# A hybrid decoder step in split fp32: halves of the seven-product matmul regrouped, state transposes and forget loads moved

## What is computed

```
x = x + 0.5 * SwiGLU1(RMSNorm(x))          # (silu(x @ w_gate) * (x @ w_up)) @ w_out, hidden width 2816
h = RMSNorm(x); z = h @ w_in               # q|k|v|forget logits, RG-LRU inputs, short-conv inputs, 3 branch gates
o_a = forgetting attention (prompt causal; sample with a paged cache of 256 keys and cached log-forgets)
o_b = RG-LRU over time * gelu(...)         # also returns its last state and its conv window
o_c = gated short convolution              # also returns its conv window
merged = sum_b sigmoid(g_b) * (o_b @ W_branch_b);  x = x + merged @ w_out
x = x + 0.5 * SwiGLU2(RMSNorm(x))
```

## Time and profile before

| | |
|---|---|
| median of 3 runs | 2904.15 us (2902.32 to 2904.93) |
| profiled execution | 2909.55 us |
| its span | 2907.9 us |
| granted clock of TensorE, mean | 0.998 |
| PE busy | 2837.9 us (98%), 21280 matmuls |
| DVE busy | 1708.7 us (59%) |
| ACT busy | 1131.7 us (39%) |
| POOL busy | 312.1 us (11%) |
| share of the chain that ended last | PE 88%, DVE 5%, issue 3% |

### The profile page before, as it was taken

One profiled execution on the slowest core, in us unless ns is written; L12 is line 12 of the kernel. 1 busy time (PEld: TensorE's weight loads), 2 busy tenths in 40 slices (PEclk: granted clock), 3 DMA queues, 4 the chain that ended last, 5 costly groups with the idle time before them and its releaser, 6 DMA issues.

```text
span 2907.9 us, 56195 instructions
## 1 busy us (share of the span) xinstructions
PE 2837.9 (98%) x21280; PEld 2770.5 (95%) x21280; DVE 1708.7 (59%) x2441; ACT 1131.7 (39%) x1683; POOL 312.1 (11%) x232
## 2 busy tenths in 40 slices
PE   7999999999999999999999999999999999999999
PEld 6999999898899999999999999998889999999998
DVE  4565746676645446656547565576665544474754
ACT  4332323555633333333333333335554333342324
POOL 1120201000000011111102021100000001030201
PEclk9999999999999999999999999999999999999999
DMA  3222223333222222222222223233332222223222
GB/s 120 72 89 87 88 72 99 90 93 89 81 80 87 87 84 68 95 72 96 79 81 81 88 73 100 75 89 90 89 109 67 79 87 94 73 74 101 73 87 91
DMA packets 299061, 249.22 MB, mean 86 GB/s; under 512 B 20644, under 2 KB 296308, under 8 KB 298920
## 3 DMA queue, kind: packets, MB, share of 16 engines
q1 hardware_dynamic: 296775, 242.44, 26.9%
q0 software_dynamic: 2144, 4.98, 0.5%
HBM read 240.04 MB, written 7.34 MB: 85 GB/s over the span
## 4 chain that ended last, share of the span: by engine, by line
PE 88%; DVE 5%; issue 3%; SPq 1%; DVEq 1%; ACT 1%; DMA 1%; POOLq 0%; ACTq 0%
PE ps L508 72%; PE ps L550 8%; DVE bl L1260 1%; PE ps L710 1%; DVE wlo L1251 1%; PE ps L650 1%; PE ps L649 1%; PE ps L648 1%; PE ps L728 1%; PE ps L690 1%; SPq L426 1%; DVE tmp L1225 1%; SPq L424 1%; PE ps L775 0%; PE ps L697 0%
## 5 line engine op out<-in xcount | busy, mean ns | idle before, releaser
L508 PE MATMUL ps<-hh,whi 128*128 128x288 f32 x4480 | 967.9, 298 | 14.2 <-DVE wlo L1219 8.1
L508 PE MATMUL ps<-hh,wlo 128*128 128x288 f32 x4480 | 961.3, 296 | 0.0
L508 PE MATMUL ps<-hl,whi 128*128 128x288 f32 x4480 | 961.1, 296 | 0.0
L875 ACT ACTIVATE whi<-wraw 128x1024 fp32r<-128x1024 f32 (+1 forms) x388 | 403.8, 1041 | 1144.4 <-PE ps L508 1118.0
L508 PEld LDWEIGHTS ps<-hh,whi 128*128 128x128 f32 x4480 | 724.1, 189 | 17.8 <-DVE wlo L1219 6.1
L508 PEld LDWEIGHTS ps<-hl,whi 128*128 128x128 f32 x4480 | 723.8, 189 | 0.0
L508 PEld LDWEIGHTS ps<-hh,wlo 128*128 128x128 f32 x4480 | 723.7, 189 | 0.0
L1219 DVE TENSOR_TENSOR wlo<-wraw,whi 128x1024 fp32r<-128x1024 f32 (+1 forms) x388 | 466.8, 1203 | 388.5 <-ACT whi L875 387.7
L1268 DVE TENSOR_TENSOR tmp<-tmp,ps 128x576 f32<-128x576 f32 x128 | 96.4, 753 | 343.9 <-PE ps L508 343.5
L550 PE MATMUL ps<-bh,whi 128*128 128x288 f32 x896 | 267.0, 298 | 23.0 <-DVE wlo L1251 18.9
L550 PE MATMUL ps<-bh,wlo 128*128 128x288 f32 x896 | 266.7, 298 | 0.0
(11 more groups left out here) (333 smaller groups left out, 3607.5 us busy)
## 6 DMA issues: line engine op xcount, KB each, us to landing
wraw<-in_ffn_w_in SPq DMA_DIRECT2D x88, 1024.0 KB
wraw<-in_ffn_w_out SPq DMA_DIRECT2D x32, 1024.0 KB
wraw<-in_w_in SPq DMA_DIRECT2D x28, 1024.0 KB
wraw<-in_w_in SPq DMA_DIRECT2D x56, 512.0 KB
wraw<-in_ffn_w_out SPq DMA_DIRECT2D x16, 768.0 KB
wraw<-in_w_branch SPq DMA_DIRECT2D x24, 512.0 KB
wraw<-in_w_out SPq DMA_DIRECT2D x9, 1024.0 KB
kv<-in_cache_k SPq DMA_DIRECT2D x128, 64.0 KB, 1.8
```

What stands on the lines that cost most here:

```text
L508: last = pe.matmul(ps[slot][:, half, 0:HF], weights, rhs[:, k, half * HF:(half + 1) * HF], start=(start and c == 0 and n == 0), stop=(stop ...
L875: act.activation(split_tile(into, j, rowwise), raw_tile(slot, j, rowwise), ACT.Copy).then_inc(hi_ready, 1)
```

## The change

Four edits go together. (1) The halves of K become even and odd chunks, so block kk of all seven moving operands is made in step i = kk: k=2 gives B11, B12, T1 (light), k=3 the rest (heavy), in every step. `kept` shrinks from four blocks to one. Weight blocks are cut from `wraw` to match. PE now waits for each block kk in all products of u=0. (2) ACT rounds block 3 ahead of the products instead of between them. (3) The stage `state` stands behind `merge`; ACT and DVE make `oh` and `ol` of four chunks ahead of each branch of the first merge step, which is written out ahead of a loop over the other three. `fout` moves to memory of its own. (4) `past_forgets` stands in part three of ffn1, between its w_in loads and its w_out loads.

```diff
+MOVED = {M_B11: 1, M_T1: 1, M_T2: 2, M_T3: 2, M_B21: 3, M_B22: 3, M_T4: 4}
...
+    s["merge"] = Stage(plan, 4, 6, 12)
     s["state"] = Stage(plan, 1, 0, 1)
-    s["merge"] = Stage(plan, 4, 6, 12)
...
-            return wraw[:, u, :].rearrange("p (k c) -> p k c", c=256)[:, 4 * kh:4 * kh + 4, mh_ * P:mh_ * P + P]
+            return wraw[:, u, :].rearrange("p (k h c) -> p h k c", h=2, c=256)[:, kh, :, mh_ * P:mh_ * P + P]
...
                         load(st_in, 1, L, i, (w1, 0, KD, i * 256 + (done * P + FFN), 256))
+                    if name == "ffn1" and kc == 6:
+                        past_forgets(L)
                     with sp.Fori(0, 2) as i:
                         for k in range(2):
                             load(st_out, k, L, i, (w2, done, kc, i * 512 + 256 * k, 256))
-                    if name == "ffn1" and done == 0:
-                        past_forgets(L)
...
-                        if q == 0:
-                            pe.wait_ge(mov_ready, L * 64 + (16 * g + 4))
...
-                            if u == 0 and m >= 2:
-                                pe.wait_ge(mov_ready, L * 64 + (16 * g + 4 + 3 * kk + (1 if x_ in (M_T2, M_T3) else 3 if x_ == M_T4 else 2)))
+                            if u == 0:
+                                pe.wait_ge(mov_ready, L * 64 + (16 * g + 4 * kk + MOVED[x_]))
...
+            def moving_first(g, kk, L):
+                act.wait_ge(mov_raw, L * 48 + (12 * g + 3 * kk + 1))
+                act.activation(bh[:, M_B11:M_T1 + 1, kk, :], kept[:, 0:3:2, :], ACT.Copy).then_inc(mov_hi, 1)
+
+            def moving_second(g, kk, L):
+                act.wait_ge(mov_raw, L * 48 + (12 * g + 3 * kk + 2))
                 act.activation(bh[:, M_T2:M_T3 + 1, kk, :], two(tmp[2][:, 0:N]), ACT.Copy).then_inc(mov_hi, 1)
+                act.activation(bh[:, M_B21:M_B22 + 1, kk, :], two(tmp[5][:, 0:N]), ACT.Copy).then_inc(mov_hi, 1)
+                act.wait_ge(mov_raw, L * 48 + (12 * g + 3 * kk + 3))
                 act.activation(bh[:, M_T4, kk, :], tmp[3][:, 0:HF], ACT.Copy).then_inc(mov_hi, 1)
...
-                        elif c < 4:
-                            moving_early(g, c, L)
-                        elif c < 7:
-                            moving_sums(g, c - 4, L)
-                            moving_late(g, c - 4, L)
+                        elif k == 2:
+                            moving_first(g, i, L)
+                        else:
+                            moving_second(g, i, L)
...
-                        if q == 1:
-                            moving_late(g, 3, L)
...
-                        if q == 0:
-                            moving_sums(g, 3, L)
...
+                def merge_step(i, first):
                     for b in range(3):
+                        if first:
+                            split_merged(b)
...
+                merge_step(0, True)
+                with act.Fori(1, mg.steps) as i:
+                    merge_step(i, False)
+                st = S["state"]
+                wait_tile(st, 0, L)
+                act.activation(frow[:, :], ps[st.slot(0)][0:NO, 0, :], ACT.Copy).then_inc(freed[st.slot(0)], 1)
```

More of the change, by code:

```diff
@@ L182, in build @@
         small = sb("small", [P, 64])
+        fout = sb("fout", [P, 4, NO])
         tmp = [sb(f"tmp{i}", [P, UB + 1]) for i in range(7)]
@@ L195, in build @@
             bl = sb("bl", [P, 7, 4, HF], F32R, m)
-            kept = sb("kept", [P, 4, 3, HF], F32, m)
+            kept = sb("kept", [P, 3, HF], F32, m)
             wsum = sb("wsum", [P, 4, 4 * P], F32, m)
@@ L817, in _ @@
                     last.then_inc(filled[pr.slot(23)], 1)
[L820 to L825, removed]
                 mg = S["merge"]
@@ L835, in _ @@
                             plain(mg, 4 * b + j, 4 * b + j, range(4 * b, 4 * b + 4), oh, ol, L, i)
+                st = S["state"]
+                pe.wait_ge(f_ready, L + 1)
+                wait_apart(pe, freed[st.slot(0)], st.turn(0, L))
+                for t in range(4):
+                    last = pe.transpose(ps[st.slot(0)][0:NO, 0, t * P:(t + 1) * P], fout[:, t, :], ident)
+                last.then_inc(filled[st.slot(0)], 1)
                 with pe.Fori(0, 2) as i:
@@ L1170, in _, with split_merged @@
                 act.drain()
-                st = S["state"]
-                wait_tile(st, 0, L)
                 act.wait_ge(f_ready, L + 1)
-                for c in range(12):
-                    act.activation(oh[:, c, :], o[:, c, :], ACT.Copy).then_inc(oh_ready, 1)
-                act.activation(frow[:, :], ps[st.slot(0)][0:NO, 0, :], ACT.Copy).then_inc(freed[st.slot(0)], 1)
                 mg = S["merge"]
-                with act.Fori(0, mg.steps) as i:
+                def split_merged(b):
+                    for c in range(4 * b, 4 * b + 4):
+                        act.activation(oh[:, c, :], o[:, c, :], ACT.Copy).then_inc(oh_ready, 1)
+                def merge_step(i, first):
                     for b in range(3):
+                        if first:
+                            split_merged(b)
                         for j in range(4):
@@ L1271, in gates_seven @@
                             continue
[L1272 removed]
                         dve.drain()
                         dve.wait_ge(silu_ready, L * 44 + (s0 + i * 2 + k - 1))
[L1275 to L1276 removed]
+                        if k == 2:
+                            dve.tensor_tensor(kept[:, 0:2, :], two(pf[:, 0:N]), two(tmp[0][:, 0:N]), ALU.mult)
                             dve.drain()
[L1278 to L1280 removed]
+                            dve.tensor_tensor(kept[:, 2, :], kept[:, 1, :], kept[:, 0, :], ALU.subtract).then_inc(mov_raw, 1)
+                            if i < 3:
+                                split_ahead(st, k, L, i)
+                            else:
+                                comb_split(st_out, g, 0, L)
+                                comb_split(st_out, g, 1, L)
+                            moving_lo(g, i, 1, M_B11, M_T1 + 1, kept[:, 0:3:2, :], L)
                             continue
[L1282 to L1283 removed]
+                        dve.tensor_tensor(pf[:, 0:N], pf[:, 0:N], tmp[1][:, 0:N], ALU.mult)
                         dve.drain()
[L1285 to L1286 removed]
+                        dve.tensor_tensor(tmp[2][:, 0:HF], pf[:, HF:N], kept[:, 2, :], ALU.subtract)
+                        dve.tensor_tensor(tmp[2][:, HF:N], pf[:, HF:N], kept[:, 1, :], ALU.subtract).then_inc(mov_raw, 1)
                         dve.drain()
@@ L1677, in _, with split_merged, merge_step @@
                 dve.wait_ge(k_stored, L * (PAIRS * 32) + PAIRS * 32)
-                for c in range(12):
-                    dve.wait_ge(oh_ready, L * 12 + (c + 1))
-                    dve.tensor_tensor(ol[:, c, :], o[:, c, :], oh[:, c, :].bitcast(F32), ALU.subtract).then_inc(o_ready, 1)
                 mg = S["merge"]
-                with dve.Fori(0, mg.steps) as i:
+                def split_merged(b):
+                    for c in range(4 * b, 4 * b + 4):
+                        dve.wait_ge(oh_ready, L * 12 + (c + 1))
+                        dve.tensor_tensor(ol[:, c, :], o[:, c, :], oh[:, c, :].bitcast(F32), ALU.subtract).then_inc(o_ready, 1)
+                def merge_step(i, first):
                     for b in range(3):
+                        if first:
+                            split_merged(b)
                         for j in range(4):
@@ L1710, in _ @@
                                 dve.tensor_tensor(chunk(ml, c), chunk(merged, c), chunk(mh, c).bitcast(F32), ALU.subtract).then_inc(m_ready, 1)
+                merge_step(0, True)
+                with dve.Fori(1, mg.steps) as i:
+                    merge_step(i, False)
                 update(S["out"], L, 1.0, 16, L, 16)
```

37 lines of the change are left out of this document (9 added, 28 removed).

## The result

The changed kernel takes **2884.04 us** (median of 4 runs, 2880.72 to 2886.48) against 2904.54 (median of 4, 2902.32 to 2905.26), a ratio of 0.992 with a 95% interval of 0.9908 to 0.9932. It was forecast at 2885, within 2877 to 2893, and it is 20.5 us faster where the sum said 19.3. The profiled execution is one of the four: 2886.48, span 2884.8. The ratio and the two medians are not the same estimate: 0.992 of 2904.54 would be 23.2 us less, and the interval reaches from 19.8 to 26.7.

A forecast was written before the change was run, and what follows sets the result against it. PE, busy 98% of the span, was taken as the bound, so gains come only from its waits or low clock; 5.3 + 10.8 + 3.2 = 19.3 us off median 2904.15 gave 2884.9, said as 2885, range 2877 to 2893.

The forecast's parts named there:

- Halves, 0.66 a stage, 5.3: Seven-product stages: DVE starts the last gate tile 0.66 us earlier, so product 4 comes earlier; 5.3 us over eight stages.
- The swallowed delay: Seven-product stages: a delay at product 2, perhaps 0.15 us, is absorbed before product 4, as would be up to 1 more.
- POOL's sum beside product 3's low part: Seven-product stages: product 3's low part on DVE stays slowed by POOL's sum, 1.79 instead of 0.68; the 1.1 us stay.
- Rival 2: Seven-product stages: POOL's sum no longer meets product 3's low part, 1.1 us a stage more gained; 2876 us, chance 0.07.
- State behind merge, 5.4 a layer, 10.8: Merge start: wait 3.4, transposes 0.45 and slow clock about 1.6 go; 5.4 us a layer, 10.8 in two.
- e2's rival: Merge start: low clock stays without the idle stretch, only wait and transposes go; some 7.3 us, 2897; no chance given.
- The 1.6 of low clock: First merge tile: the low clock behind PE's idle time goes with the wait, about 1.6 us a layer.
- Forget loads, 3.2: First tile of part two: PE's 1.56 us wait and a 0.1 restart go, 1.65 a layer; 3.2 us in two.
- The sum: Whole kernel: 5.3 + 10.8 + 3.2 = 19.3 us gained, from median 2904.15 to 2884.9.
- 1: Seven-product stages: the regrouping gives nothing, the copy behind three roundings holds product 2, product 4 comes no earlier; 2890, chance 0.17.
- 3: A part fails: low clock appears elsewhere, or forgets delay their new place by 1 to 2 us; 2888 to 2889, chance 0.10.
- 4: Products 0 and 1: block 3 of B11 and T1 comes too late and they wait; slower, 2915 us, chance 0.02.

The follow-up runs named there:

- e1: The kernel before with only the even and odd halves and their order on DVE, ACT and PE; 2902.7 us, ratio 0.9981.
- e4: The kernel after with ACT's copy of product 0 put ahead of the last block's roundings; 2887.35 us, ratio 0.9929.
- e5: The kernel after with POOL's second sum for the second weight unit held until all moving operands' low parts are made; 2878.66 us, ratio 0.9892.
- e2: The kernel before with only the state stage moved behind the merge stage; 2896.81 us, ratio 0.9968.
- e7: The kernel before with PE's wait ahead of the state transposes filled by 14 dummy identity matmuls, no work moved; 2904.58 us, ratio 0.9976.
- e3: The kernel before with only the past forget loads moved to their new place in the feed-forward stage; 2903.32 us, ratio 0.9987.
- e8: The kernel of e6 with POOL's first sum for the third weight unit also held back by two low parts; 2872.46 us, ratio 0.9879.
- e9: The kernel after, unchanged, run on the same chip as e8; 2887.3 us, ratio 0.9928.
- e6: The kernel after with the edits of both e4 and e5; 2879.7 us, ratio 0.9900.

## Why the prediction was right, point by point

- **Halves, 0.66 a stage, 5.3.** Right in mechanism. DVE reached the last gate tile 0.66 earlier relative to PE (0.20 behind the stage's first matmul, not 0.86); the loss fell from 3.36 to 2.61 a stage, 0.75, or 6.0 in eight. e1 alone gave 5.5. Product 2 was placed at about 143.0 from a start of 138.04, and is at 142.88 from 137.94: 0.15 more lost than before, as said. Here two small errors cancelled. The copy ended 0.25 sooner after the stage's start than the prediction had it (142.65 against 143.0, with the starts 0.10 apart), and the prediction left out the 0.23 that PE then takes to go on, which it had read at the low parts as 0.22.
- **The swallowed delay.** Right: e4 took 0.86 away at product 2, and only 0.07 of it reached the end of the stage.
- **POOL's sum beside product 3's low part.** Right: it stayed, at 1.77 beside a sum of 1.66, and it ends 0.55 after that sum does, as the Trainium skill has it (SBUF — State Buffer, Who interferes with whom: a DVE instruction with two SBUF inputs and a GpSimd instruction that reads SBUF exclude each other, and the later one is blocked). What I didn't say is that the pair of `bl` behind it is slowed by the next sum as well, by 1.1. Together these 2.2 us were more than product 4's whole wait, and e5 got that wait back. Rival 2 had the first slowdown right (1.1) but took all of it as gained. PE gets back only product 4's 0.86 a stage, 6.9 in eight and not 8.8, and the change alone doesn't bring that; one added wait does.
- **State behind merge, 5.4 a layer, 10.8.** Right to 0.02 us in the trace (13.33 a layer against 13.35 foreseen). The third merge tile was not late, and the transposes fitted into the wait for `ml`, which fell from 1.00 to 0.6. e2 alone measured 9.3, with 5.8 to 12.8 as its interval, so the time alone could not have told 10.8 from the 7.3 of e2's rival; the trace does. The 1.6 of low clock within the 5.4 was the riskiest term; e7 gives 1.5 for it.
- **Forget loads, 3.2.** Right. The w_out load is 5.2 late (said: 5.7), and ACT doesn't notice. The prediction took the second layer to be like the first, untested: there the wait was 1.39 instead of 1.56, and the first tile of part two follows without one now. The two borders lost 1.7 and 1.6. e3 alone: 3.8 (1.2 to 6.4).
- **The sum.** 6.0 + 10.8 + 3.3 are 20.1 by the trace; the medians differ by 20.5, and by 20.5 again in the repeat beside e8 (2907.76 against 2887.3, both some 3 us higher). That 2884.04 lies 1 us from the forecast is thus partly luck, and the difference is what was foretold. The profiled executions differ by more, 23.1 in span. Some 1.7 of that is a stretch of low clock at the border of the layers, which the profiled run of the kernel before has and that of the kernel after has not. The windows 1462 to 1486 of before and 1451 to 1475 of after have clocks of 0.93 and 1.00, and 24 x 0.07 is 1.7. No part of the change was made to remove it: e4, which has the whole change, shows it again (0.93 in 1452 to 1476), while e1, without the moved state, doesn't (1.00). It comes and goes. The 20.1 and these 1.7 leave 1.3. The two programs' matmuls account for about that: in three stretches of some 20 us each (925 to 945, 2232 to 2252, 2347 to 2365) those of the kernel after follow each other in 0.130 us instead of 0.133, with the same clock of 1.00, which is 1.4 us in all, and the profiled run of the kernel before has no such stretch. It is no effect of the change either: e9, the same program as the kernel after, has its 1.4 at other places (35 to 39 and 991 to 1041). The last section has more on it.
- **The rivals.** 1, 3 and 4 fall: product 4 did come earlier, nothing was late at the new places, the clock of the profiled run has no new low stretch there, and no product waits for block 3.

## What to carry to other kernels

When several waits stand in a row, find the one resource that sets the last of them. Taking away an earlier wait alone gives nothing (e4), and taking away the last one alone gives only its own size (e5). Then look some microseconds further, where the work that was pushed aside lands: e6 lost there what e4's edit should have given, and one more held-back instruction, found in the trace, brought it back. A wait of TensorE can cost more than its length (1.5 us more for 3.2 here), and dummy matmuls in it gave that back (e7).

## What the runs showed of the hardware

- **The low clock behind a wait is not a fixed price.** The wait of 3.2 us cost 1.5 us of low clock in the kernel before, 2.3 in e3 and 2.5 in e1 (14.85, 15.64 and 15.85 against 13.35 with the wait filled). Shorter waits cost it sometimes: near 48 us the kernel before waits 2.68 and the clock stays at 1.00, e1 waits 1.99 and has 0.57 in 48 to 52:

```profile
47.96 0.61 PE L509 MATMUL ps<-hh,whi 128*128 128x288 f32 x2 [1.99 <-DVE wlo L1210]
48.37 0.68 PE L509 MATMUL ps<-hl,whi 128*128 128x288 f32 x2
48.85 0.68 PE L509 MATMUL ps<-hh,wlo 128*128 128x288 f32 x2
```

  Pairs that take 0.27 from start to start elsewhere take 0.48 here. A stretch such as the one at the layers' border costs about 1.7 us, and the kernel before has a run-to-run spread of some 10 us (2902 to 2912 over the comparisons). Such stretches are only a part of it: every run has its mean granted clock on record, and of the 43 runs of the kernel before beside e1 to e9 the 11 with a clock of 0.997 took 2909.1 us on average and the 7 with 0.999 took 2906.6, while the 24 with 0.998 reach from 2902.3 to 2910.8. The next point is another part; how much of the spread the two make up together isn't measured.
- **At full clock, too, matmuls come at two spacings.** The programs of e5 and e6 differ little from the sixth seven-product stage to the seventh, yet that takes 850.6 us in e5 and 847.3 in e6. The windows 2480 to 2520 of both, e5 first, show the same granted clock and 303 matmuls against 310:

```profile
2480.00:2520.00 40.00, 40.00 (x303) 40.00 (x302) 21.08 (x28) 12.53 (x17) 0.00 (x0) 1.00 0.26 80
2480.00:2520.00 40.00, 40.00 (x310) 40.00 (x309) 21.63 (x30) 12.54 (x17) 0.00 (x0) 1.00 0.26 81
```

  From start to start a matmul of 288 columns takes 0.133 us for most of each run, and 0.130 in stretches of 20 to 90 us: 1.4 us gained in the profiled run of the kernel after, 2.2 in e3, 2.7 in e2, 5.5 in e6 (where it more than makes up for the two stretches of low clock), about 0.1 in the kernel before, e1, e4, e5 and e7. They do not lie at the same places in all runs. What brings them isn't known. So two single profiles of this kernel should not be compared to better than a few microseconds unless both the clocks and the counts of matmuls are laid side by side.
- **DVE can also be the one that blocks.** In e5 and e6 POOL's held-back sum began while DVE ran low parts back to back, and took 2.06 and 2.67 instead of the 1.3 to 1.7 of the others in that stage; DVE's low parts at that time kept to 0.6 to 0.7 each.
